# Summing the squares of the attention heads by accumulating activations instead of one square and a reduction

## The reference

```python
a = p[:, :, 0] - lam * p[:, :, 1]             # p: two softmaxes of each head
d_out = einsum('bhqk,bkhd->bqhd', a, v)       # 128 values per head
d_out = rms_norm(d_out, diff_norm_g) * (1.0 - lam_init)   # over the 128 values of a head
```

## Time and profile before

| what | value |
|---|---|
| time, median of 3 runs | 1486.17 us (1485.14 to 1489.09) |
| profiled execution, own time | 1489.09 us |
| its span | 1487.4 us |
| mean granted TensorE clock | 0.986 |
| busy share TensorE, VectorE, ScalarE | 97%, 86%, 68% |

### The profile page before, as it was taken

How to read it: one execution, slowest core, us unless ns; L and a number is a source line. 1 busy time by engine, 2 the same in 40 slices (tenths; PEclk the granted TensorE clock), 3 DMA queues, 4 the chain that set the end, 5 groups by cost and what they waited for, 6 DMA issues and landing times.

```text
span 1487.4 us, 21906 instructions
## 1 busy us (share of the span) xinstructions
PE 1438.4 (97%) x6777; PEld 1181.7 (79%) x6777; DVE 1280.3 (86%) x1125; ACT 1016.8 (68%) x874; POOL 233.7 (16%) x238
## 2 busy tenths in 40 slices
PE   7999899599999999999999999999999999999996
PEld 6888578478888888888888888888888888888884
DVE  5465847699999999999999999999999999999997
ACT  5424724367777777777777777777777777777774
POOL 0100301411111111111111111211111111121112
PEclk9999989799999999999999999999999999999998
DMA  9442100799999999999999999999999999999994
GB/s 341 181 176 115 44 0 37 243 333 355 366 368 368 364 371 364 378 365 371 374 367 366 386 349 368 380 372 368 365 372 372 366 369 365 377 367 369 370 370 162
DMA packets 131534, 471.98 MB, mean 317 GB/s; under 512 B 15380, under 2 KB 15672, under 8 KB 131320
## 3 DMA queue, kind: packets, MB, share of 16 engines
q1 hardware_dynamic: 118016, 450.94, 80.8%
q0 software_dynamic: 13168, 20.16, 5.5%
q10 hardware_dynamic: 328, 0.60, 0.1%
HBM read 467.96 MB, written 32.51 MB: 336 GB/s over the span
## 4 chain that ended last, share of the span: by engine, by line
PE 91%; DVE 4%; issue 2%; DMA 1%; ACT 1%; POOL 0%; POOLq 0%; DVEq 0%; SPq 0%; ACTq 0%
PE pair L979 24%; PE pair L981 23%; PE pair L987 23%; PE pair L700 3%; PE pair L701 3%; PE pair L705 3%; PE pair L1005 2%; PE pair L993 2%; PE pair L955 2%; PE pair L839 1%; PE pair L840 1%; PE pair L852 1%; DVE split L1806 1%; DMA expert_sums<-work,list_cur 1%; PE pair L792 0%
## 5 line engine op out<-in xcount | busy, mean ns | idle before, releaser
L1806 DVE TENSOR_TENSOR split<-ring,split 128x2048 fp32r<-128x2048 f32 x396 | 892.0, 2288 | 74.3 <-ACT split L1288 74.3
L1288 ACT CAST split<-ring 128x2048 fp32r<-128x2048 f32 x396 | 758.4, 1916 | 201.2 <-PE pair L987 192.1
L979 PE MATMUL pair<-split,operands 128*128 128x512 f32 x1584 | 630.5, 398 | 0.0
L981 PE MATMUL pair<-split,operands 128*128 128x512 f32 x1584 | 618.5, 390 | 0.0
L987 PE MATMUL pair<-split,operands 128*128 128x512 f32 x1584 | 424.4, 390 | 0.0
L987 PEld LDWEIGHTS pair<-split,operands 128*128 128x128 f32 x1584 | 297.3, 188 | 63.2
L979 PEld LDWEIGHTS pair<-split,operands 128*128 128x128 f32 x1584 | 298.1, 188 | 58.8
L981 PEld LDWEIGHTS pair<-split,operands 128*128 128x128 f32 x1584 | 298.2, 188 | 58.6
L2045 POOL DMA_INDIRECT expert_sums<-work,list_cur x32 | 61.1, 1910 | 470.2 <-PE pair L987 438.8
L2038 POOL DMA_INDIRECT work<-h_rows,token_next x35 | 70.3, 2009 | 190.3 <-DMA token_next<-slot_lists 156.6
L1294 ACT CAST operands<-pair 128x512 fp32r<-128x512 f32 x66 | 38.7, 588 | 68.3 <-PE pair L987 41.4
(11 more groups left out here) (258 smaller groups left out, 1144.4 us busy)
## 6 DMA issues: line engine op xcount, KB each, us to landing
ring<-in_w_moe_in SPq DMA_DIRECT2D x264, 1024.0 KB, 9.1
ring<-in_w_moe_out SPq DMA_DIRECT2D x132, 1024.0 KB, 10.5
ring<-in_w_in SPq DMA_DIRECT2D x12, 1024.0 KB, 10.5
ring<-in_w_o SPq DMA_DIRECT2D x4, 1024.0 KB, 10.3
resid<-in_x SPq DMA_DIRECT2D x4, 512.0 KB, 5.4
expert_sums<-zero_rows SPq DMA_DIRECT2D x4, 512.0 KB, 11.7
work<-expert_sums SPq DMA_DIRECT2D x4, 512.0 KB, 5.4
out<-ring SPq DMA_DIRECT2D x4, 512.0 KB, 2.6
```

The lines of the kernel that those rows point to most:

```text
L979: pe.matmul(dst[:, f, :], left_hi[:, k0 + k, :], hi[c.buffer][:, k, cols], start=(start and k == 0), stop=False)
L981: pe.matmul(dst[:, f, :], left_lo[:, k0 + k, :], hi[c.buffer][:, k, cols], start=False, stop=False)
L1288: act.copy(hi[c.buffer], raw[c.slot]).then_inc(hi_made, 1)
L1806: dve.tensor_tensor(lo[c.buffer], raw[c.slot], hi[c.buffer].bitcast(F32), ALU.subtract).then_inc(lo_made, 1)
```

## The change

The squares of a tile's four heads are now taken by four activations that read bank 6 directly, scale by row_rec on the way in and accumulate their sum, one per head. They stand ahead of the row copy. sum_squares, the products by row_rec and three semaphores are gone; one semaphore, row_scale_ready, tells that row_rec of a tile is there. The early Sqrt is gone. ScalarE's loop is written anew: in step s it does exponentials(s), then the copy of unit s-2 (before: of unit s-1), and the tile's squares and row copy in step s = 4i+6 (before: 4i+5).

```diff
                 for h in range(NH):
                     col = 16 + 2 * NH * i + first_head + h
+                    if first_head == 0:
+                        chain(act.activation(square_tmp[:, h, :], outputs[h], ACT.Square, scale=row_rec[:, i, h:h + 1],
+                                             accum_out=stat[:, col:col + 1]))
+                    else:
+                        chain(act.activation(square_tmp[:, h, :], outputs[h], ACT.Square,
+                                             accum_out=stat[:, col:col + 1]))
...
-            for s in range(1, NU + 2):
+            for s in range(NU + 3):
                 if 2 <= s < NU:
                     exponentials(s)
-                if s == NU:
-                    act.activation(stat[:, 55:56], eps_col[:, 0:1], ACT.Sqrt).then_inc(root_table, 1)
-                if s - 1 < NU:
-                    turned_map(s - 1)
-                if s >= 5 and (s - 5) % NH == 0:
-                    att_rows((s - 5) // NH)
-
-            act.wait_ge(squares_scaled, 1)
+                if 2 <= s < NU + 2:
+                    u = s - 2
+                    n = (u // NH + 1) * P
+                    act.wait_ge(att_transposed, u + 1)
+                    if u >= 2:
+                        act.wait_ge(av_ready, u - 1)
+                    act.copy(attT[:, u % 2, 0:n], bank[4 + u % 2][:, 0:n]).then_inc(attT_ready, 1)
+                if s >= 3 and (s - 3) % NH == NH - 1:
+                    i = (s - 3) // NH
+                    act.wait_ge(av_ready, s - 2)
+                    act.wait_ge(row_scale_ready, i + 1)
+                    head_squares([bank[6][:, h * P:(h + 1) * P] for h in range(NH)], i, 0)
+                    act.copy(mix[:, i, 0:512], bank[6]).then_inc(av_evicted, 1)
+
+            chain.settle()
...
                 if u % NH == NH - 1:
-                    chain(dve.reciprocal(row_rec[:, u // NH, :], row_sum[:, u - NH + 1:u + 1, 0]))
-
-            def sum_squares(i):
-                dve.wait_ge(att_squared, i + 1)
-                dve.tensor_reduce(head_stat[:, i, 0:NH], square_tmp, AX_X, ALU.add).then_inc(squares_summed, 1)
+                    dve.reciprocal(row_rec[:, u // NH, :], row_sum[:, u - NH + 1:u + 1, 0]).then_inc(row_scale_ready, 1)
...
-                if s >= 7 and (s - 7) % NH == 0:
-                    sum_squares((s - 7) // NH)
-
-            sum_squares(NT - 1)
-            dve.wait_ge(squares_summed, NT)
-            for n in range(2):
-                chain.settle()
-                ins = dve.tensor_tensor(head_stat[:, :, 0:NH], head_stat[:, :, 0:NH], row_rec[:, :, :], ALU.mult)
-                if n == 0:
-                    chain(ins)
-            ins.then_inc(squares_scaled, 1)
```

More of the change, by code:

```diff
@@ L365, in build @@
         bias_ready = sem("bias_ready")
-        squares_summed = sem("squares_summed")
-        squares_scaled = sem("squares_scaled")
-        att_squared = sem("att_squared")
+        row_scale_ready = sem("row_scale_ready")
         exp_done = sem("exp_done")
@@ L1187, in head_squares @@
                     col = 16 + 2 * NH * i + first_head + h
-                    chain(act.activation(square_tmp[:, h, :], outputs[h], ACT.Square,
-                                         accum_out=stat[:, col:col + 1]))
+                    if first_head == 0:
[4 more added lines that the diff above has]
+                                             accum_out=stat[:, col:col + 1]))
@@ L1191, in _ @@
             chain = Chain(act, act_step)
             NU = NT * NH
[L1195 to L1209, removed]
@@ L1225, in ret_squares @@
             def ret_squares(i):
-                if i == 0:
-                    act.wait_ge(squares_summed, NT)
                 act.wait_ge(ret_out, i + 1)
```

## The result

The changed kernel takes 1500.5 us (median of 5 runs, 1493.18 to 1501.35) where the kernel before takes 1485.16 (5 runs, the three of the table among them, 1484.98 to 1489.09). The ratio is 1.0084, with a 95% interval of 1.0061 to 1.0106. It is slower, as forecast, but by 15.3 us by the medians, not 5.5, and outside the range. All 32 runs on record of the changed kernel lie from 1492.43 to 1503.27 us, median 1499.6, in two groups: 9 at 1492.4 to 1495.6 at a mean clock of 0.984 to 0.987, and 21 at 1498.1 to 1503.3 at 0.978 to 0.982, with two between. Both of its profiles are of the second group. In the experiments one run of the version with scores first took 1620.36 us at a mean clock of 0.844; it is left out of that version's figures.

What follows compares the result with a forecast made beforehand. Bound: a loop through ScalarE, VectorE and TensorE in the attention heads, ending at decay(0), 192.23 us. Its delay of 4.7 to 5.8, taken as 5.5, plus the median 1486.2 gave 1491.7 us (profiled 1489.1 to 1494.6); range 1487.5 to 1496.5.

Steps and rivals of the forecast that it cites:

- The order of the work: Attention heads: later attT copy and squares ahead of the row copy delay decay(0) by 4.7 to 5.8 us, 5.5 taken.
- The end of the tile of 384: Attention heads, change of tile from 384 to 512: 6.92 us, so the first 512-wide exponential starts near 178.4 instead of 175.19.
- pitch of the squares: ScalarE: with a scale pointer one square follows another after 0.35 us, so four hold it for 1.40 us.
- four gaps: TensorE idle for about 2 us before a tile's first att_values at each of four tile ends, released by the row copy.
- the table load covered: ScalarE behind the last row copy: load and root, some 1.6 us, cost nothing; ready by about 196.5, needed about 200.4.
- qd early: Stage tail on VectorE: qd products 2.4 us earlier gain nothing by themselves, as decay(0) then waits for TensorE's scores.
- I leave that slow stretch where it is: Half clock from 198.3 to 208.5 us, behind the stage, assumed to stay in place relative to the work; nothing added.
- The forecast's own last sign of being wrong: Whole forecast fails if granted clock differs by a stretch between the two profiles, which weighs as much as the edit.
- Rival 2: Idle time at tile ends makes the clock fall inside the attention stage too: about 4 us more, 1495.8; chance 0.16.
- Rival 3: Attention stage: squares cost 0.26 us each or VectorE partly absorbs ScalarE's delay: 3.2 to 4.3 us, 1489.4 to 1490.5; chance 0.20.
- Rival 5: Attention stage: VectorE's queue decides, TensorE never waits for the bank 6 copy; 4.2 us faster, 1482.0; chance 0.06.
- Rival 4: The slow clock stretch at 198.3 us disappears, winning 5.1 us against the 5.5: 1486.6; chance 0.06.

Runs made afterwards that it cites:

- the version with scores first: Kernel before with qd products ahead of the last sum, last sum and row_rec products behind decay(1), two ret_score ahead of ret_kvs: 1489.66 us, ratio 1.0027.
- the fillings: Changed kernel with 16 unused transposes ahead of each of the four av_evicted waits: 1498.86 us with the identity; with rows of x, seven runs, 1488.9 to 1498.4.
- both filled profiles: The version with scores first, and both moves undone, each with the products of ret_output(0) done three times over: 1484.68 and 1488.66 us.
- both moves undone: Changed kernel with row copy ahead of the squares, which read it in SBUF, and ScalarE's unit order as before: 1493.87 us, ratio 1.0054.
- the kernel with ScalarE's order undone: Changed kernel with attT copy, squares and row copy one step earlier, as before; squares still ahead of the row copy: 1488.33 us, ratio 1.0023.
- the kernel with the copy first: Changed kernel with the row copy ahead of the four squares, which then read mix; all else as changed: 1494.91 us, ratio 1.0066.

## Why the prediction was wrong, by its own steps

- **The order of the work: right.** The sum gave 4.7 to 5.8 us for the delay of decay(0), 5.5 taken. With the clock held up by the fillings it is 5.7 to 5.8 us in four profiles. The end of the tile of 384 fits too: the first 512-wide exponential starts at 179.3 us in the filled kernel, where 178.4 was forecast; with the falls it starts at 182.6. Its parts hold as well: pitch of the squares 0.35 us, four gaps of 1.9 to 2.3 us, the table load covered (the root was there at 202.0 us, VectorE came to it at 206.9), qd early and then a wait of 3.17 us for L772.
- **"I leave that slow stretch where it is": this step failed.** It failed in two ways. First, the sum took a stretch as part of the kernel before that most of its runs don't have; against the usual run it is 4.6 us to the worse when it comes. The sign stood in the table: the profiled execution was 2.9 us above the median of the runs, and I added 5.5 to both. Second, in the changed kernel the stretch is in both profiles: rest 101.4 and 103.1 us, 4.8 and 6.5 us over 96.6. So a term that the sum put at nothing is 4.8 to 6.5 us. The forecast's own last sign of being wrong, that the clock differs by a stretch between the profiles, came true.
- **Rival 2, falls inside the stage: it happened, and had 0.16.** Three falls in one profile, two in the other, which made the stage 5.0 and 2.5 us longer than the filled 43.0 us. The 4 us worked out for it lie between. What was wrong is the chance, and that it was treated as alone: the stretch behind came on top of it.
- The parts add up. First profile: 5.7 + 5.0 + 4.8 = 15.5 us over a usual run of before; second: 5.7 + 2.5 + 6.5 = 14.7. The medians differ by 15.3.
- **Rival 3**, cheap squares or a delay that VectorE absorbs, 3.2 to 4.3 us, is refuted by the pitch and by the 5.7 us of the filled stage. **Rival 5** overlooked, as the forecast said it would, that TensorE waits for the row copy in all four places. **Rival 4** had it the wrong way round: the stretch is missing from most runs of before and is there in both profiles of the changed kernel.

**What stays open.** That the idle time matters is shown by the fillings: inside the stage four filled profiles have no fall where the two unfilled ones have three and two; behind it the stretch went from both filled profiles, and with both moves undone all ten filled runs (1486.6 to 1489.7 us) lie below all seven unfilled ones (1491.9 to 1495.2). The profiled filled run, at 1489.66, is the slowest but one of the ten and has no stretch. That idle time isn't all is shown by pairs of profiles with the same idle time and a different clock. That its place in time is the other half fits the delays and is not shown apart from them. Which time is bad was not worked out. In the kernel with ScalarE's order undone the gap ahead of ret_kvs is wider, 2.27 us, yet the profile has no stretch and only one of ten runs a mean clock of 0.984 or less; the kernel with the copy first has 0.88 us there and four of four runs at 0.982 to 0.983. Nothing shown here explains that.

## What to carry to other kernels

A reordering that costs 6 us of waits in a stage that hands TensorE short pieces can cost 15, since idle time there can be followed by half the clock for the next 3 to 14 us, also in a stage that was not touched. Before a sum is made against a profiled execution, compare its time with the other runs: where it lies above their median, take a second profile and look for the stretch that the others lack. The mean clock over the whole kernel would not have told it here. To tell waits from clock, fill the idle time with products that nothing uses and profile again; and judge a change of a few microseconds ahead of a dense stretch by several runs, since it also moves the work in time.

## What the runs showed of the hardware that had not been expected

- Moving work in time by 1 to 4 us changed the kernel's time out of proportion, once with the other sign: the kernel before delayed by 1.7 us, +7.3 us; delayed by 3.5 us, +4.4 us; its tail made 1.3 us shorter, +4.8 us (1489.66 to 1484.87).
- The same share of busy time, 9.65 of 12.00 us with two delays and 7.40 and 7.41 of 9.70 us in two executions of one kernel, was followed by 1.2 GHz in one execution and by 2.4 GHz in the other. Idle gaps of 2.0 us at one tile end were followed by a fall in one execution and not in the next.
- A stretch of 1.2 GHz behind the stage lasted 10.2 to 13.7 us, with TensorE busy throughout, before the clock rose again; inside the stage it lasted 3.4 to 6.8 us.
- The stage's start followed the time from which the clock was full at the beginning of the kernel: 154.9 us for 17.5, 156.1 for 19.7, 156.7 for 20.5.
